# Sample attention on TensorE over padded 32-column blocks, with the cache shift copies in SyncE's queue

## The reference

```
h = x + W_out(concat[A(xn), B(xn), C(xn)]),  xn = RMSNorm(x), one input projection W_in
y = h + PEER(RMSNorm(h))          # 8 heads, 16 of 16384 single-neuron experts each
```

```
idx = lb + arange(t)[:,None] - arange(n_off+1)[None,:]*dil      # n_off = window // dil = 128
g = concat([kv_buf, kv_new])[:, idx]
logits = einsum('bthd,btkhd->bthk', q, g.k) * SCALE + bias
lse = logsumexp(logits); o = einsum('bthk,btkhd->bthd', exp(logits - lse), g.v)
```

## Time and profile before

| | us |
|---|---|
| median of 3 runs | 2049.31 |
| lowest and highest run | 2048.93, 2054.47 |
| the profiled execution | 2055.78 |
| its span, first to last instruction | 2053.6 |
| TensorE busy in the span | 1678.3 |
| DVE busy | 1162.0 |
| POOL busy | 694.6 |
| ACT busy | 592.6 |

### The profile page before, as it was taken

How to read it: one execution, slowest core, us unless ns; L and a number is a source line. 1 busy time by engine, 2 the same in 40 slices (tenths; PEclk the granted TensorE clock), 3 DMA queues, 4 the chain that set the end, 5 groups by cost and what they waited for, 6 DMA issues and landing times.

```text
span 2053.6 us, 16891 instructions
## 1 busy us (share of the span) xinstructions
PE 1678.3 (82%) x5096; PEld 877.2 (43%) x5096; DVE 1162.0 (57%) x2773; ACT 592.6 (29%) x1828; POOL 694.6 (34%) x686
## 2 busy tenths in 40 slices
PE   6985999998788777777789759999887878777777
PEld 4653875543333333223146557655333333332221
DVE  1454038786776776444435331668777767744544
ACT  2231014342333423222322211334333333322222
POOL 2112003455444344334300120244544534443332
PEclk8887699999899989999999858999989999899999
DMA  5598269999999999999947965699999999999997
GB/s 177 212 379 308 85 244 376 420 407 420 421 420 420 420 420 421 420 420 421 421 180 278 379 218 203 242 402 416 417 420 420 419 421 420 420 421 420 421 421 289
DMA packets 104564, 742.25 MB, mean 361 GB/s; under 512 B 14859, under 2 KB 15958, under 8 KB 23704
## 3 DMA queue, kind: packets, MB, share of 16 engines
q0 software_dynamic: 92480, 640.11, 76.2%
q1 hardware_dynamic: 9684, 56.63, 7.4%
q10 hardware_dynamic: 2308, 44.43, 5.7%
HBM read 736.76 MB, written 48.20 MB: 382 GB/s over the span
## 4 chain that ended last, share of the span: by engine, by line
DMA 45%; PE 39%; DVE 9%; ACT 3%; issue 2%; DVEq 1%; ACTq 1%; POOL 0%; SPq 0%; POOLq 0%
DMA arena<-peer_uv,idx 28%; PE bank L1401 17%; DMA qf<-peer_uv,idx 7%; PE bank L1372 6%; PE bank L1268 4%; PE bank L1501 3%; PE bank L1263 3%; PE bank L1487 3%; DMA scores<-qrows 3%; DVE arena L1095 2%; DMA yt<-peer_uv,idx 2%; DMA wring<-peer_uv,idx 2%; DMA wring<-w_col 2%; DMA wring<-w_tok 1%; PE bank L1356 1%
## 5 line engine op out<-in xcount | busy, mean ns | idle before, releaser
L1401 PE MATMUL bank<-arena,diag 128*128 128x512 f32 (+1 forms) x1456 | 708.4, 632 | 169.5 <-ACT diag L697 169.4
L534 POOL DMA_INDIRECT arena<-peer_uv,idx x364 | 397.4, 1092 | 706.1 <-PE bank L1401 463.5
L1095 DVE SCALAR_TENSOR_TENSOR arena<-arena,xn 128x1024 f32<-128x1024 f32 x364 | 441.3, 1225 | 305.5 <-DMA arena<-peer_uv,idx 303.8
L1401 PEld LDWEIGHTS bank<-arena,diag 128*128 128x128 f32 (+1 forms) x1456 | 269.9, 191 | 577.1 <-issue 317.5
L689 ACT ACTIVATE act<-hid 128x2 f32<-128x2 f32 x288 | 58.6, 203 | 882.3 <-DVE arena L1095 542.3
L1401 PE MATMUL bank<-wring,diag 128*128 128x512 f32 (+1 forms) x352 | 174.8, 636 | 41.8 <-ACT diag L697 41.8
L697 ACT ACTIVATE diag<-ident,weight 128x128 f32<-128x128 f32 (+1 forms) x576 | 194.7, 385 | 20.4 <-issue 0.7
L1268 PE MATMUL bank<-xt,wring 128*128 128x288 f32 x512 | 142.9, 438 | 48.8 <-DVE yt L987 29.0
L1401 PE MATMUL bank<-qf,diag 128*128 128x512 f32 (+1 forms) x304 | 149.9, 631 | 40.1 <-ACT diag L697 40.1
L692 ACT ACTIVATE weight<-act,gate 128x1 f32<-128x1 f32 x576 | 138.4, 287 | 20.4 <-issue 0.7
L1095 DVE SCALAR_TENSOR_TENSOR wring<-wring,xn 128x1024 f32<-128x1024 f32 x88 | 106.7, 1224 | 58.1 <-DMA wring<-peer_uv,idx 57.6
(11 more groups left out here) (230 smaller groups left out, 1537.9 us busy)
## 6 DMA issues: line engine op xcount, KB each, us to landing
kvs<-cache_a_kv_w ACTq DMA_DIRECT2D x16, 2044.0 KB, 14.0
wring<-w_col SPq DMA_DIRECT2D x16, 1024.0 KB, 8.5
qf<-cache_rows POOLq DMA_DIRECT2D x24, 576.0 KB, 8.3
wring<-w_tok SPq DMA_DIRECT2D x8, 1408.0 KB, 10.0
arena<-peer_wq SPq DMA_DIRECT2D x10, 1024.0 KB, 9.1
wring<-w_out SPq DMA_DIRECT2D x8, 1024.0 KB, 5.2
kvs<-cache_a_kv_w ACTq DMA_DIRECT2D x16, 508.0 KB, 8.0
scores<-qrows POOLq DMA_DIRECT2D x8, 768.0 KB, 14.6
```

What stands on the lines that cost most here:

```text
L534: pool.indirect_dma_start(out=ring[j], out_offset=None, in_=io["peer_uv"], in_offset=bass.IndirectOffsetOnAxis(ap=idx[:, n:n + 1], axis=0) ...
L1095: last = v.scalar_tensor_tensor(out=ring[j][:, 0:D], in0=ring[j][:, 0:D], scalar=1.0, in1=xn[:, i, :], op0=ALU.mult, op1=ALU.mult, accum_o ...
L1401: last = pe.matmul(bank[b0 + half][0:r, :], diag[:, n % 16, 0:r], ring[SLOT_OF[n]][:, D + 512 * half:D + 512 * half + 512], start=False, s ...
```

## The change

Keys and values of the caches are laid out on the host as two arrays; the keys with the head's numbers on the partitions. For each sequence 9 blocks of 128 x 128 (4 of the group of 512, 4 of 2048, 1 of 128) are now the moving operand, and the stationary one is a window of 32 columns in which only the columns of the right token and head are not zero. The windows overlap in two buffers of 2400 columns, `qz` (queries, written by DVE's `query_windows`) and `pz` (probabilities, written by ACT), which POOL clears in each layer. The four sequences of a half add into the same 32 rows of one PSUM bank, so that the logits stand there as 64 rows (token and head) of 3 x 160, and the softmax over all groups is one maximum, one exponential with its sum, one reciprocal and one product. The query rows' way over DRAM, `key_dots`, the turning of their sums and the second softmax's old form are gone. Value matmuls go between u1, u2 and `mix`; ACT copies their sums, TensorE turns them, ACT writes `yt`. POOL loads seven key blocks at once, then each value block when the key matmuls of that place are done.

The shift copies move from ACT to SP: 24 parts a layer (two halves of the 2048 group, then the two small ones, for each sequence), one or two of them right behind each weight chunk 2 to 17, cut in rows of some 8 KB. `conv_taps` and `conv_keep` stand ahead of `mixed` on DVE. The samples' bias is built for 64 rows.

```diff
--- before.py
+++ after.py
...
+        kc = [flat_qf[:, b * 9 * P:(b + 1) * 9 * P].rearrange("p (c n) -> p c n", c=9) for b in range(4)]
+        kc += [cand[:, 0:9 * P].rearrange("p (c n) -> p c n", c=9), scores[:, 0:9 * P].rearrange("p (c n) -> p c n", c=9), tail, kc[0]]
+        vc = [flat_xn[:, 0:9 * P].rearrange("p (c n) -> p c n", c=9)] + kc[1:]
...
+            def shift(l, m):
+
+                b, part = m // 3, m % 3
+                for (win, _), src, dst, rows in zip(GROUPS, ("cache_a_kv_w128", "cache_a_kv_w512", "cache_a_kv_w2048"),
+                                                    ("kvs128", "kvs512", "kvs2048"), (16, 64, 256)):
+                    if (win == 2048) == (part == 2):
+                        continue
+                    d_ = io[dst].rearrange("l b r k h d -> l b (r k h d)")[l, b, 0:(win - NT) * 256].rearrange("(q n) -> q n", q=rows)
+                    s_ = io[src].rearrange("l b r k h d -> l b (r k h d)")[l, b, NT * 256:win * 256].rearrange("(q n) -> q n", q=rows)
+                    if win == 2048:
+                        d_, s_ = d_[P * part:P * part + P], s_[P * part:P * part + P]
+                    sp.dma_start(d_, s_).then_inc(shift_out, 16)
...
                     sp.wait_ge(in_ps, len(OUTS) * l + IN_DONE[c - 2])
                     load_w(l, c)
+                    for m in range(3 * (c - 2) // 2, 3 * (c - 1) // 2):
+                        shift(l, m)
...
-                for b in range(4):
+                for b in range(NB - 1):
                     load_k(l, b)
+                if l:
+                    pool.wait_ge(xs_ps, 6 * l)
+                pool.memset(flat_xn[:, 0:2400 + NG * 2 * NS], 0.0).then_inc(qz_clear, 1)
...
+                pool.wait_ge(key_ps, NB * l + 1)
+                load_k(l, NB - 1)
+                pool.wait_ge(qk_done, 6 * (l + 1))
+                pool.memset(pz, 0.0).then_inc(pz_clear, 1)
+                for b in range(1, NB - 1):
+                    pool.wait_ge(key_ps, NB * l + b + 1)
+                    load_v(l, b)
+                pool.wait_ge(key_ps, NB * (l + 1))
+                load_v(l, 0)
+                load_v(l, NB - 1)
...
+            def sample_prob_copy(l):
+
+                a.wait_ge(probt_ps, 3 * l + 1)
+                a.wait_ge(pz_clear, l + 1)
+                src = pts_ps.rearrange("p g (a h m) -> p g a h m", a=2, h=2)
+                for h in range(2):
+                    near = pz[:, 0:8 * 36].rearrange("p (a b w) -> p a b w", a=2, b=4)[:, :, :, 16 * h:16 * h + NT]
+                    a.activation(near, src[:, 0, :, h, :].rearrange("p a (b t) -> p a b t", t=NT), ACT.Copy)
+                    far = pz[:, 8 * 36:2400].rearrange("p (g a m w) -> p g a m w", g=2, a=2, m=16)[:, :, :, :, 16 * h]
+                    a.activation(far, src[:, 1:3, :, h, :], ACT.Copy)
+                a.activation(ptn[0:NS, :, :], ptn_ps, ACT.Copy).then_inc(probt_done, 1)
...
+            def query_windows(l):
+
+                v.drain()
+                v.wait_ge(qz_clear, l + 1)
...
+                    near = qz[r, 0:8 * 36].rearrange("p (a b w) -> p a b w", a=2, b=4)[:, :, :, 16 * h:16 * h + NT]
+                    v.tensor_copy(near, qt[r, 0, SEQ:TOKENS].rearrange("p (a b t) -> p a b t", a=2, b=4))
+                    far = qz[r, 8 * 36:2400].rearrange("p (g a m w) -> p g a m w", g=2, a=2, m=16)[:, :, :, :, 16 * h]
+                    v.tensor_copy(far, qt[r, 1:3, SEQ:TOKENS].rearrange("p g (a m) -> p g a m", a=2))
+                    all_ = qblk[r].rearrange("p g (a h m) -> p g a h m", a=2, h=2)[:, :, :, h, :]
+                    last = v.tensor_copy(all_, qt[r, :, SEQ:TOKENS].rearrange("p g (a m) -> p g a m", a=2))
...
+            def sample_max(l):
+
+                v.wait_ge(logit_ps, 3 * l + 1)
+                v.scalar_tensor_tensor(out=lgs[0:2 * NS, :, :], in0=slog, scalar=SCALE, in1=sbias[:, :, :],
+                                       op0=ALU.mult, op1=ALU.add).then_inc(slog_read, 1)
+                v.drain()
+                v.tensor_reduce(smax[0:2 * NS, :], lgs[0:2 * NS, :, :].rearrange("p g n -> p (g n)"), AX.X, ALU.max,
+                                negate=True).then_inc(max_done, 1)
+
+            def sample_share(l):
+
+                v.wait_ge(exp_done, 3 * l + 1)
+                v.reciprocal(stot[0:2 * NS, :], stot[0:2 * NS, :])
+                v.drain()
+                v.tensor_scalar(lgs[0:2 * NS, :, :], lgs[0:2 * NS, :, :], stot[0:2 * NS, :], None, ALU.mult).then_inc(prob_done, 1)
...
+            def windows_of(buf, b):
+
+                a, b4 = b // 4, b % 4
+                near = near_windows(buf)[:, a, NS * b4:NS * b4 + NS]
+                far = [[far_windows(buf)[:, g, a, NS * (NT * b4 + t):NS * (NT * b4 + t) + NS] for t in range(NT)] for g in range(2)]
+                return slice(NS * a, NS * a + NS), near, far
+
+            def sample_keys(l, b):
+
+                if b == 0:
+                    pe.wait_ge(qz_done, l + 1)
+                pe.wait_ge(k_in[b], 16 * (l + 1))
+                r, near, far = windows_of(qz, b)
+                pe.matmul(slog[r, 0, 0:P], near, kc[b][:, 8, :], start=(b % 4 == 0), stop=False)
+                for t in range(NT):
+                    for g in range(2):
+                        last = pe.matmul(slog[r, g + 1, 0:P], far[g][t], kc[b][:, 4 * g + t, :], start=False, stop=False)
+                last.then_inc(key_ps, 1)
...
+            def turn_sample_probs(l):
+
+                pe.wait_ge(prob_done, 3 * l + 1)
+                for g in range(NG):
+                    pe.transpose(pts_ps[:, g, :], lgs[0:2 * NS, g, 0:P], ident[0:2 * NS, 0:2 * NS])
+                    last = pe.transpose(ptn_ps[:, g, :], lgs[0:2 * NS, g, P:P + NS], ident[0:2 * NS, 0:2 * NS])
+                last.then_inc(probt_ps, 1)
+
+            def new_values(l):
+
+                pe.wait_ge(probt_done, 3 * l + 2)
+                for g in range(NG):
+                    pe.matmul(pv_ps[:, g, :], ptn[0:NS, g, :], kvn[:, 1, g * P:(g + 1) * P], start=(g == 0), stop=False)
+
...
+            def sample_values(l, b):
+
+                pe.wait_ge(v_in[b], 16 * (l + 1))
+                r, near, far = windows_of(pz, b)
+                pe.matmul(pv_ps[r, 0, :], near, vc[b][:, 8, :], start=False, stop=False)
+                for t in range(NT):
+                    for g in range(2):
+                        last = pe.matmul(pv_ps[r, g + 1, :], far[g][t], vc[b][:, 4 * g + t, :], start=False, stop=(b in (0, NB - 1) and t == NT - 1 and g == 1))
...
-                    pe.wait_ge(row_copied, 2 * l + 2)
-                    pe.wait_ge(new_read, l + 1)
+                    pe.wait_ge(row_copied, l + 1)
+                    pe.wait_ge(slog_read, l + 1)
                 else:
-                    pe.wait_ge(max_done, 3 * l + 1)
+                    pe.wait_ge(max_done, 3 * l + 2)
+                    pe.wait_ge(probt_done, 3 * l + 1)
...
                 out(l, "k1")
-                sample_rows(l, 1)
                 out(l, "k2")
                 qk_mean(l, 3)
                 qk_mean(l, 4)
+                for b in range(0, 3):
+                    sample_keys(l, b)
                 out(l, "AS")
                 qk_mean(l, 5)
+                for b in range(3, 5):
+                    sample_keys(l, b)
                 out(l, "BS")
+                for b in range(5, NB):
+                    sample_keys(l, b)
+                sample_rows(l)
+                new_logits(l)
                 out(l, "xb0")
-                sample_rows(l, 2)
-                new_logits(l)
                 out(l, "gc0")
+                turn_sample_probs(l)
                 logits(l, 1)
                 out(l, "xb1")
                 out(l, "gc1")
                 logits(l, 0)
                 out(l, "T1")
-                turn_probs(l, 0, 1)
+                turn_probs(l, 1, 1)
                 out(l, "T2")
                 out(l, "u1")
-                values(l, 0, 1)
+                values(l, 1, 1)
+                new_values(l)
+                for b in range(1, 5):
+                    sample_values(l, b)
                 out(l, "u2")
-                turn_probs(l, 1, 0)
+                turn_probs(l, 2, 0)
+                for b in (5, 6, 0, 7):
+                    sample_values(l, b)
                 pe.wait_ge(vc_done, 2 * (l + 1))
                 if l == 0:
                     pe.wait_ge(mix_ready, 1)
                 mix(l, 0)
                 mix(l, 1)
                 mix(l, 2)
+                turn_sample_values(l)
                 out(l, "gb0")
-                values(l, 1, 0)
+                values(l, 2, 0)
...
```

More of the change, by code:

```diff
@@ L1287, in new_logits @@
             def new_logits(l):
-                pe.wait_ge(qk_done, 6 * (l + 1))
-                for h in (0, 2, 4, 1, 3, 5):
-                    r = slice(64 * (h % 2), 64 * (h % 2) + 64)
-                    last = pe.matmul(new_ps[h % 2][:, h // 2, :], qt[r, h // 2, SEQ:TOKENS], kt[r, h // 2, SEQ:TOKENS], start=True, stop=True)
```

(2 more changed lines are left out.)

287 lines of the change are left out of this document (109 added, 178 removed).

## The result

The changed kernel takes 1955.49 us (median of 4 runs, 1953.06 to 1955.82); the kernel before, run on the same chip, 2051.14 us. The ratio is 0.953, with a 95% interval of 0.9512 to 0.9547: 4.7% faster. The profiled execution took 1955.55 us, its span 1953.8; against the profiled execution before (2055.78, span 2053.6) that is 100.2 us less.

The account below looks back on a forecast made before the run. Memory bounds the gathers; order, not work, bounds the stage before the output projection. New stage 68.9 + 31.6 + 1.8 = 102.3 us; gains 95.3 us, so 2055.8 - 95.3 + 3 = 1963.5, against the median 1957; range 1930 to 2000.

Parts of the forecast that it names:

- The bound and the stage: From the end of k2 to the output projection: bound by order, not work; new length 68.9 + 31.6 + 1.8 = 102.3 us.
- The kept work: TensorE instructions that remain between the end of k2 and the output projection, summed to 68.9 us a layer.
- the tail: End of the stage, at gb1: an ACT copy and two DVE products, 1.8 us before and after.
- The price of a block: Padded key and value matmuls: 0.11 us an instruction, 144 instructions each a layer, 15.8 us for keys and 15.8 for values.
- The rival in which blocks overlap: Padded matmuls at 0.077 us each, 9.5 us a layer less: 1938 us; overlap or fewer gaps, under 1945, chance 0.15.
- The clock under the blocks: Full clock in padded key and value matmuls; rival of half clock, 20 to 31 us more a layer, 1997 to 2020, chance 0.09.
- The 2.7 us kept for the mixing matmuls' half clock: The product behind the mixing matmuls took 6.65 us in place of 4.0; this loss was expected to stay.
- The output projection: It starts warm, saving 2.0 and 2.65 us; its first 48 instructions take 11.64 us at full clock.
- What was to stay hidden: Sample softmax covered by xb0 and gc0, else 4 us a layer; window copies and GpSimd clearings (2.9, 2.5 us) also off the path.
- SP's queue: Copies following each weight chunk fit, 40 MB or 103 us a layer up to the output projection; priced at 3 us over the run.
- The DMA pieces of 9.07 and 19.52 us in the old chain: Layer 1 before the output projection: read as waits for a token chunk and a column chunk.
- Late chunks: Rival: beside key or value loads SP's row gets half of 390 GB/s; 24 us more, 1981 us, up to 2000; chance 0.2.

## Why the prediction was right, and where its steps were off

**The bound and the stage.** The forecast built the new stage from TensorE's own instructions, 102.3 us, and the trace has 100.2 in both layers: 94.2 us won where 89.9 were forecast. Three terms make up the 2.1 us in layer 1. The blocks took 28.7 us by themselves and not 31.6: some key blocks ran beside the second token product (1.8 us), and blocks of one half beside those of the other where the samples' order changes the half (1.0 us); the forecast had put such overlap at nothing. The kept work took 69.8 us and not 68.9 (its ten products at 8.03/2 are 40.2 us, where the sum has 39.7), the tail 1.7 and not 1.8. The price of a block, the least certain term, came to 0.109 us an instruction against 0.11, and for the reason given: alternating between two groups of output partitions brought 0.055, between four 0.029. The rival in which blocks overlap was false but for 2.8 us in this order of samples, and true in another one. The Trainium skill states the mechanism, in TensorE: Matmul & The Clock Gate, Part 3 on packing small matmuls: matmuls on different 32-wide tiles of the array run concurrently, and the output's start partition picks the column tile. The runs agree with that. They don't agree with the sentence there that weight loads overlap running matmuls only on other row groups: all blocks here use all 128 rows, and the loads of 110 ns were hidden once the column groups differed.

**The clock under the blocks** stayed at 1.00, as taken from the product on 32 weight columns; doubling the keys did not change it. The 2.7 us kept for the mixing matmuls' half clock were there, 6.99 in place of 4.08, and the run with value blocks between them had them back.

**The output projection** took 11.88 us for its first 48 instructions, not 11.64, and brought 4.2 us (4.65 forecast); the tail of gb1 took 1.70 (1.8).

**What was to stay hidden** did: the sample softmax ended by 1074.9 us and its turning began at 1079.89. GpSimd's clearings took 2.3 and 2.1 us (the first is of 2592 elements a partition, not 2784), within the 2.9 and 2.5 allowed. Its price without cover was put at 4 us a layer; it measured 6.2 in the stage, 3.0 of it idle and the rest mostly through the clock, which the forecast did not count.

**SP's queue.** The 3 us for it are not contradicted (3.1 us less without copies, within what the intervals allow). What failed is the sentence that ACT loses 24 issues of copies "which TensorE did not wait for". It took the move for a cost only. The stage of 102.3 us holds only if chunks come on time, and that is what the move brings: without it the same attention part is 42 us slower. The forecast gave all of the gain to the attention part, and the number came out right because both parts were in the change. The DMA pieces of 9.07 and 19.52 us in the old chain were the sign, though the forecast read them as waits of TensorE of that length (it stood 2.6 and 9.7 us there): not the issue of a copy on ACT held TensorE, but chunks that came late while copies were under way.

**Late chunks.** The rule of the Trainium skill that the prediction names (DMA: Bandwidth & Descriptors, section Queues, rings and completion order), with the sum of 1981 us made from it, holds in its order (a chunk behind its copies lands 3 us later) but not in its consequence: in the change a chunk stands behind the copies of the chunk before, and the some eight microseconds of products between two chunks are room enough. With three parts behind each chunk, or the copies ahead of it, the time is near the rival's 1981: 1986 and 1976 us.

**The number.** The parts of the sum missed by 4.3 us in the stages and by 3.7 in all that lies outside them and the projection (2.3 us lost forecast, 1.4 won), both the same way: 100.2 us between the profiled executions against 92.3. Between the medians the gain was 95.7 us. That 1957 us came within 1.5 us of 1955.49 is in part luck: the profiled execution before was slower than its median, and that took back most of what the parts had missed.
